# A hybrid decoder layer in float32: the column stream given out anew around the attention, and the sample products turned round

## The reference, cut to what matters

```
n = rmsnorm(x)
c_rw, c_att, c_gate = split(n @ w_in)
o_rw  = rwkv7_mix(c_rw, ...)                 # 16 heads, recurrent state per request
o_att = attend(rope(q), rope(k), v, ...)     # 8 heads, 2 key heads, top-k chosen by an indexer
h = x + (sig(g_rw) * (o_rw @ p_rw) + sig(g_att) * (o_att @ p_att)) @ w_o
gate, up = split(rmsnorm(h) @ w_up)
y = h + (silu(causal_conv(gate)) * up) @ w_down

# attention of one block: q (Q,H,D), keys and values chosen by the indexer
s = q . k * D**-0.5, masked to the chosen keys
p = softmax(s)
o = p @ v
```

## Time and profile before

| | |
|---|---|
| median of 3 runs | 1928.93 us (1928.53 to 1933.64) |
| the profiled execution | 1924.94 us, of which 1923.4 us from the first to the last instruction |
| granted TensorE clock, mean | 0.984 of full speed |
| TensorE busy | 96% of the span, 16744 matmuls |
| VectorE, ScalarE, GpSimd busy | 59%, 36%, 9% |
| HBM traffic | 147 GB/s over the span |

### The profile page before, as it was taken

One profiled execution on the slowest core, in us unless ns is written; L12 is line 12 of the kernel. 1 busy time (PEld: TensorE's weight loads), 2 busy tenths in 40 slices (PEclk: granted clock), 3 DMA queues, 4 the chain that ended last, 5 costly groups with the idle time before them and its releaser, 6 DMA issues.

```text
span 1923.4 us, 41121 instructions
## 1 busy us (share of the span) xinstructions
PE 1849.6 (96%) x16744; PEld 1759.5 (91%) x16744; DVE 1132.4 (59%) x2015; ACT 700.5 (36%) x910; POOL 168.0 (9%) x126
## 2 busy tenths in 40 slices
PE   5999989999999999999999999999999999999997
PEld 3999858998888888889999999999999999999997
DVE  4333866217777777776655666666666666344444
ACT  4333234333333333343334433333333333333332
POOL 2600325441000000000000000000000000000000
PEclk7999989999999999999999999999999999999998
DMA  4644323331222222245444544444444444544443
GB/s 180 220 162 166 110 102 110 125 139 62 103 103 103 92 92 103 99 148 175 172 154 169 218 162 166 169 158 165 162 172 155 167 160 161 209 164 164 160 162 135
DMA packets 50746, 283.49 MB, mean 147 GB/s; under 512 B 7104, under 2 KB 12160, under 8 KB 24576
## 3 DMA queue, kind: packets, MB, share of 16 engines
q1 hardware_dynamic: 43488, 260.87, 39.2%
q10 hardware_dynamic: 3072, 12.63, 1.7%
q0 software_dynamic: 4128, 9.18, 1.4%
HBM read 274.38 MB, written 8.27 MB: 147 GB/s over the span
## 4 chain that ended last, share of the span: by engine, by line
PE 80%; DVE 12%; ACT 3%; issue 2%; DMA 1%; POOL 1%; DVEq 0%; ACTq 0%; SPq 0%
PE bank L575 25%; PE bank L577 23%; PE bank L576 23%; DVE w_lo L524 1%; PE bank L907 1%; PE bank L873 1%; POOL w_lo L524 1%; DVE w_lo L532 1%; DVE squares_k L1753 1%; DVE x_raw L1555 1%; DVE y_sq L1938 1%; ACT w_hi L540 1%; DVE rope_tmp L1593 1%; DMA w_raw<-in_w_down 1%; PE bank L716 1%
## 5 line engine op out<-in xcount | busy, mean ns | idle before, releaser
L575 PE MATMUL bank<-x_split,w_lo 128*128 128x288 f32 x2944 | 907.0, 308 | 22.4 <-DVE x_split L1561 16.6
L576 PE MATMUL bank<-x_split,w_hi 128*128 128x288 f32 x2944 | 873.3, 297 | 0.0
L577 PE MATMUL bank<-x_split,w_hi 128*128 128x288 f32 x2944 | 870.7, 296 | 0.0
L540 ACT ACTIVATE w_hi<-w_raw 128x2048 fp32r<-128x2048 f32 (+1 forms) x264 | 472.4, 1789 | 573.4 <-PE bank L577 554.5
L524 DVE TENSOR_TENSOR w_lo<-w_raw,w_hi 128x2048 fp32r<-128x2048 f32 (+1 forms) x215 | 451.1, 2098 | 311.2 <-ACT w_hi L540 311.2
L575 PEld LDWEIGHTS bank<-x_split,w_lo 128*128 128x128 f32 x2944 | 556.3, 189 | 49.3 <-issue 29.8
L576 PEld LDWEIGHTS bank<-x_split,w_hi 128*128 128x128 f32 x2944 | 557.4, 189 | 4.2 <-issue 0.7
L577 PEld LDWEIGHTS bank<-x_split,w_hi 128*128 128x128 f32 x2944 | 558.5, 190 | 0.0
L575 PE MATMUL bank<-act_split,w_lo 128*128 128x288 f32 x704 | 208.9, 297 | 1.0 <-DVE w_lo L524 1.0
L576 PE MATMUL bank<-act_split,w_hi 128*128 128x288 f32 x704 | 207.9, 295 | 0.0
L577 PE MATMUL bank<-act_split,w_hi 128*128 128x288 f32 x704 | 207.3, 294 | 0.0
(11 more groups left out here) (366 smaller groups left out, 1602.5 us busy)
## 6 DMA issues: line engine op xcount, KB each, us to landing
w_raw<-in_w_up SPq DMA_DIRECT2D x88, 1024.0 KB, 4.8
w_raw<-in_w_in SPq DMA_DIRECT2D x48, 1024.0 KB, 4.9
w_raw<-in_w_down SPq DMA_DIRECT2D x64, 704.0 KB, 4.0
w_raw<-in_w_gate SPq DMA_DIRECT2D x32, 1024.0 KB, 4.8
w_raw<-in_w_p SPq DMA_DIRECT2D x16, 1024.0 KB, 4.8
w_raw<-in_w_o SPq DMA_DIRECT2D x16, 1024.0 KB, 4.8
x_raw<-in_x SPq DMA_DIRECT2D x4, 576.0 KB, 6.4
h<-in_x ACTq DMA_DIRECT2D x1, 2304.0 KB, 10.4
```

The lines of the kernel that those rows point to most:

```text
L540: actv(WHI[:, slot, 0:kt], WRAW[:, slot, 0:kt], ACT.Copy).then_inc(sem("w_hi"), 1)
L575: mm(out, wl, hi, start=first and k == ks[0], stop=False, skip_group_check=True)
L576: mm(out, w, lo, start=False, stop=False, skip_group_check=True)
L577: ins = mm(out, w, hi, start=False, stop=last and k == ks[-1], skip_group_check=True)
```

## The change

It has four parts.

1. The passes are given out anew: 5 instead of 10 behind the probabilities' transposes in each of six steps, 4 new ones inside each sample step, and 8, 4, 10 and 8 instead of 4, 2, 2 and 0 in the first pair's start.
2. A sample step's products are turned round: the probabilities (32 columns of a request) are the loaded operand, the values with both key heads (256 columns) the moving one. The four requests stand in four groups of 32 output rows. ScalarE copies the result, and two transposes on TensorE bring it into the layout that was there before.
3. ScalarE loads CPREV and CONVP after the first four output units.
4. The wait for the spill of h moves from VectorE to ScalarE's first write to XF.

```diff
-FILL_MIX, FILL_FIRST = 18, 4
-FILL_ROPE, FILL_TOPK_S, FILL_DOTS, FILL_TOPK, FILL_SCORES, FILL_SOFTMAX, FILL_P_T = 4, 24, 2, 64, 8, 9, 10
+FILL_MIX, FILL_FIRST, FILL_DECAY, FILL_BONUS = 18, 8, 4, 10
+FILL_ROPE, FILL_TOPK_S, FILL_DOTS, FILL_TOPK, FILL_SCORES, FILL_SOFTMAX, FILL_P_T, FILL_PV = 4, 24, 2, 64, 8, 9, 5, 4
...
+                for kc in range(2):
+                    for b in range(4):
+                        c0 = kc * P + 32 * b
+                        mm(BK[6][32 * b:32 * b + 32, 0:KVH * HDIM], PRT[:, c0:c0 + 32], VC[:, b, kc, :], start=kc == 0, stop=False,
+                           skip_group_check=True)
                 for b in range(4):
-                    for g in range(KVH):
-                        out = BK[6][:, (b * KVH + g) * 16:(b * KVH + g + 1) * 16]
-                        c0 = b * 32 + g * 16
-                        for kc in range(2):
-                            mm(out, VC[:, b, kc, g * P:(g + 1) * P], PRT[:, kc * P + c0:kc * P + c0 + 16],
-                               start=kc == 0, stop=False)
-                        ins = mm(out, VNEW[:, b, g * P:(g + 1) * P], PRT[0:DS, 2 * P + c0:2 * P + c0 + 16],
-                                 start=False, stop=True)
+                    c0 = 2 * P + 32 * b
+                    ins = mm(BK[6][32 * b:32 * b + 32, 0:KVH * HDIM], PRT[0:DS, c0:c0 + 32], VNEW[:, b, :], start=False, stop=True,
+                             skip_group_check=True)
+                ins.then_inc(sem("pv_tok"), 1)
+                fill_cols(FILL_PV)
+                pe.wait_ge(sem("pv_sb"), half + 1)
+                for g in range(KVH):
+                    ins = tr(BK[7][:, g * P:(g + 1) * P], PRT[:, 512 + g * P:512 + (g + 1) * P], ident)
                 ins.then_inc(sem("pv"), 1)
...
             kk_sum(1)
-            fill_cols(2)
+            fill_cols(FILL_DECAY)
             log_decay(1)
-            fill_cols(6)
+            fill_cols(FILL_BONUS)
             bonus_mm(1)
...
                 filled(FILL_P_T)
+                if kind == "sample":
+                    act.wait_ge(sem("pv_tok"), which + 1)
+                    actv(PRT[:, 512:512 + KVH * HDIM], BK[6][:, 0:KVH * HDIM], ACT.Copy).then_inc(sem("pv_sb"), 1)
+                    filled(FILL_PV)
                 act.wait_ge(sem("pv"), n + 1)
...
             o_units(0)
+            act.wait_ge(sem("merged"), KT)
+            act.dma_start(CPREV[:], a["conv_prev"]).then_inc(sem("cprev_in"), 16)
+            act.dma_start(CONVP[:], a["conv_params"]).then_inc(sem("convp_in"), 16)
...
                     act.wait_ge(sem("up_out"), g * 2 + (j + 1))
+                    if isinstance(g, int) and j == 0:
+                        act.wait_ge(sem("h_spilled"), 16)
...
-            dve.wait_ge(sem("h_spilled"), 16)
-            dve.wait_ge(sem("x_split"), 4 + KT)
             dve.wait_ge(sem("cprev_in"), 16)
```

More of the change, by code:

```diff
@@ L1272, in _ @@
                     c0 = SEQ + 16 * which
-                    for b in range(4):
-                        ins = actv(COLS[:, T_Q:T_Q + AH, c0 + DS * b:c0 + DS * b + DS],
-                                   BK[6][:, b * 32:b * 32 + 32].rearrange("p (h t) -> p h t", t=DS), ACT.Copy)
+                    for g in range(KVH):
+                        own = BK[7][:, g * P:(g + 1) * P].rearrange("p (b g h t) -> p b g h t", b=4, g=KVH, t=DS)[:, :, g]
+                        q = COLS[:, T_Q + 4 * g:T_Q + 4 * g + 4, c0:c0 + 16].rearrange("p h (b t) -> p b h t", t=DS)
+                        ins = actv(q, own, ACT.Copy)
                     ins.then_inc(sem("o_sb"), 1)
@@ L1424, in _ @@
             act.dma_start(h_spill, H[:].rearrange("p k n -> p (k n)")).then_inc(sem("h_spilled"), 16)
-            act.dma_start(CPREV[:], a["conv_prev"]).then_inc(sem("cprev_in"), 16)
-            act.dma_start(CONVP[:], a["conv_params"]).then_inc(sem("convp_in"), 16)
             norm_root(1, HRSTD)
```

## The result

The changed kernel takes 1918.52 us (median of 5 executions, 1917.41 to 1921.10) against 1930.85 us for the kernel before in the same session. One of those five executions of the kernel before took 5055.87 us; the other four have a median of 1929.89, and the ratio leaves the slow one out. The ratio is 0.994, 95% interval 0.9924 to 0.9955: faster by 0.6%, more than the 0.3% that can be told. The profiled execution is the slowest of the five, 1921.1 us with a span of 1919.5 and a mean granted clock of 0.982, where the other four have 0.985. A good part of this text is about that difference between two answers.

What follows compares the result with a forecast made beforehand. The prediction took TensorE, busy 1849.6 of 1923.4 us, as the bound. Savings of 22.0 less losses of 17.6 gave -4.4, rounded to -4.6: 1920.3 for a profiled execution, 1924.3 against the median, range 1914 to 1932.

Steps and rivals of the forecast that it cites:

- no change: Whole kernel: measured time within 0.3%, 5.8 us, of the kernel before; chance 0.48.
- Sample products: Two sample steps: old products' 18.1 us become 2 x 2.35, products 2.1 and transposes 0.25 each; saved 13.4 (6.2 to 14.8).
- Clock: Sample steps, passes behind them and first pair's start: TensorE no longer drops below full clock; saved 4.4 us.
- Fewer passes behind the transposes: Attention steps: five passes, 2.0 us, still cover ScalarE's copy of the probabilities; lost at most 0.3 us.
- The first pair's start: Extra passes cover TensorE's waits of 1.2 us for squared keys and 2.4 us for the r·k product; saved 3.6.
- The LoRA wait: First LoRA product: weights load late behind GpSimd's unit 47 split, counted from A, TensorE's last sample step end; lost 13.8 us.
- The hold of the difference: First pair: VectorE's difference waits for GpSimd's subtraction until A+7.0; rival that it isn't held: 4.1 us shorter chain, chance 0.12.
- Restart: TensorE after the long idle time at the first LoRA product: low clock for 5.0 us; lost 2.5 us.
- End of the pair's start: Behind the first pair's start: GpSimd's late subtraction of unit 48 holds up VectorE's last operands; lost 1.0 us (0 to 4.6).
- Convolution: Up projection: earlier loads and the moved spill wait remove TensorE's wait there; saved 0.6 us.
- from the profiled execution to the median: Whole kernel: profiled execution lies 4.0 us below the median, so forecast 1920.3 becomes 1924.3.
- the main point: First pair: moved passes shift a unit end in ScalarE's order, delaying the LoRA weights; TensorE waits 13.8 us (12.7 to 14.9).

Runs made afterwards that it cites:

- The quarters: Changed kernel with GpSimd's subtractions of units 46, 47 and 48 each split into four instructions of a quarter: 1921.1 us.
- the three others with the old products and the list unpadded: Kernel before unchanged, 1928.94 us; kernel before with only the passes given out anew, 1940.61; kernel before with only the convolution's loads and spill wait moved, 1927.58.
- the kernel before with the longer list: Kernel before with 336 already satisfied waits (168 instructions) added at the start of TensorE's list: 1924.83 us, ratio 0.997.
- both padded kernels: Already satisfied waits added at TensorE's start: changed kernel with 88 more instructions, 1922.96 us; kernel before with 168 more, 1924.83 us.
- the products alone: Kernel before with only the sample products turned round, passes and convolution as before: 1911.46 us, ratio 0.9901.
- old passes with an early load: Changed kernel with passes given out as before and GpSimd's first-pair LoRA load waiting only for the last attention products: 1908.14 us, ratio 0.989.

## Why the prediction was right, and where only by luck

The prediction, 1924.3 within 1914 to 1932, holds the result, 5.8 above it. The effect it forecast, 4.6 us, is less than half of the 10 to 12 by which the medians differ; it gave "no change" 0.48 and "faster", which came, 0.40. Against the profiles it looks better: its terms sum to -4.4 (the -4.6 has no source of its own) and the profiles differ by -3.9. Term by term:

- **Sample products** (saved 13.4 at 2.1 us a step): 1.56 us a step, so with 0.25 for the transposes 18.1 - 3.6 = 14.5. The nearest row, the indexer's four at a time, was the right one; its 0.71 us include four tiny products, and a group of four takes 0.50 to 0.56 without them, near the low end.
- **Clock** (4.4): granted 1.00 in both steps and behind them, as forecast. In the first pair's start the restart took the place of the old low clock.
- **Fewer passes behind the transposes** (0.3): no wait for `prob` in a prompt step. The waits for GpSimd's `w_lo` grew by 0.4, to 2.0.
- **The first pair's start** (3.6): both waits are gone.
- **The LoRA wait** (13.8): 14.6. Counted from A = 407.83, the steps came at A+2.3 (split 46; forecast 2.4), A+7.0 (GpSimd; 7.0), A+10.9 (activations; 11.0), A+13.0 (split 47; 13.3), A+17.6 (GpSimd; 17.9) and A+22.7 (landing; 20.6 to 22.8). TensorE stood there at A+8.1 (7.9). The load took 5.0 us, near the median of the earlier trace rows, not the 2.7 of the earlier trace rows. The hold of the difference until A+7.0, taken from one stalled operation, was right: it took 5.33 instead of 1.08 us. The Trainium skill, "SBUF — State Buffer", section "SBUF: two separate sides", says that whichever of the two engines starts first keeps the shared ports for its whole instruction; the trace agrees, GpSimd having started 0.20 us earlier. The quarters show the two taking turns when both have work queued.
- **Restart** (2.5): 7.1 us at 1.2 GHz, 3.6 lost.
- **End of the pair's start** (1.0): 0.4 for `k_t`, behind the subtraction of unit 48 as forecast. The 1.6 at line 878 and the 1.7 of low clock behind it are another thing, the late landing of the shift output, which the prediction lacks.
- **Convolution** (0.6): 0.9.

The step that failed is none of these but the last one, from the profiled execution to the median: I took 4.0 us over the profile for both kernels alike. For the kernel before that was right. The changed kernel is at 1918.5, 2.6 under its own profile. The medians differ by 10.4 us (1928.93 against 1918.52), the profiles by 3.9, and the profiles show places for some 4 to 5 of these 6.5 us:

- The down projection of the kernel before took 297.3 us in the profile that I read, and 299.2 to 300.0 in the three others with the old products and the list unpadded; the changed kernel's took 295.8. That is 1.9 to 2.7 us.
- The first sample step took 8.1 us there and 9.2 to 9.5 in the same three: 1.1 to 1.4.
- The changed kernel's profile is its slowest execution, with the low clock of 458 to 462 us, which the two like it don't have: about 1.

These are single profiles, so the sum is an estimate. Where the lists lie has a part in it: with TensorE's list as long as before, the change gives 1922.96 against 1928.84, -5.9 (ratio 0.9966, 0.9953 to 0.9979), and against the kernel before with the longer list it gives 1918.52 against 1924.83, -6.3. The padding also shortens the start of both padded kernels by some 3 us, which makes the first of these differences too large and the second too small by as much; their mean is not touched by it. As an estimate, some 4 us of the measured gain come with the list's length, and the rest, some 6, is near the forecast of 4.6. By which steps the length acts is open.

And of the 3.9 between the profiles, 1.5 lie in the down projection, where I had nothing; up to the output projection it was 1.5 us instead of 4.0: the products brought 1.1 more than forecast, the wait cost 0.8 more, the restart 1.1, and the landing of the shift output, for which I had nothing, up to 3.3. The number was near for reasons that in part cancel, and that is luck. The mechanism of the main point is right: the products alone give 17.6 us, and the new distribution of the passes gives 11.6 of them back, through the wait that was forecast link by link.

## What to carry to other kernels

Moving filler work moves whatever other engines do at the filler's ends. Before handing passes out anew, write down which unit end falls where in ScalarE's list, and what GpSimd's in-order list holds behind it: here one unit end in another place cost a wait of 14.6 us and a restart at half clock. It moves transfers too: an output of 121.5 KB that came to lie beside two loads landed 2 us later, and TensorE waited for it. A load should stand ahead of work that it does not need, and wait for the last reader of its buffer, not for a signal that happens to be later.

Test a change part by part even when the whole is faster: here half the change was worth more than all of it, and old passes with an early load are 10.4 us better than the changed kernel.

Read two or three profiles of the kernel before, or at least its clock beside its time. One profile 4 us below the median is a particular execution, and here it showed the first sample step and the down projection too cheap.

## What the runs showed of the hardware

- Waits that were already satisfied, put at the start of TensorE's list, moved the changed kernel by +4.4 us (88 instructions) and the kernel before by -4.0 (168). The third weight load of the down projection landed in 6.8 to 9.3 us in seven profiles and in 4.0 to 5.6 in the other seven; it was late in all five that had an instruction load of 0.02 MB beside the first weight load, and in two of the nine that had not. That the one causes the other is not shown.
- After the long wait TensorE ran at 1.2 GHz for 4.5 to 7.1 us. With waits of 14.6, 13.9, 13.5 and 14.5 us it was 7.1, 6.2, 6.6 and 5.3; after 6.8 us of waiting it was 4.5, after 3.8 it was 6.0. The length of the wait did not set it.
- Products on four groups of 32 columns overlap: eight of 256 columns took 1.00 us, where four on the full array took 1.90.
- VectorE and GpSimd alternate by single instructions when both have work queued: beside GpSimd's four quarters (6.02 us) VectorE's four operations took 2.04, 1.39, 1.26 and 1.53 us, one for each quarter, where they take 1.08, 0.48, 0.25 and 0.48 undisturbed.
